# Padding the contraction of a small outer product from 32 rows to 128

## The reference

```
S_new = decay * S_old + outer(k, v_new)        # k, v_new: 128 values each, S: 128 x 128
```

## Time and profile before

| | before |
|---|---|
| median of 3 runs | 1237.82 us |
| lowest and highest | 1236.69 and 1238.21 us |
| span of the profiled execution | 1235.7 us |
| TensorE busy (weight loads) | 1207.5 us (1125.5 us) |
| VectorE, ScalarE, GpSimd busy | 793.9, 518.5, 303.2 us |
| mean granted TensorE clock | 0.995 |

### The profile page before, as it was taken

The page is one execution under the profiler, slowest core; times in us unless marked ns, Lnnn a source line. Parts: engine busy times, 40 slices in busy tenths (PEclk is TensorE's granted clock), DMA queues, the critical chain, the costliest instruction groups (busy, mean ns, idle before and its releaser), DMA issues.

```text
span 1235.7 us, 25524 instructions
## 1 busy us (share of the span) xinstructions
PE 1207.5 (98%) x8793; PEld 1125.5 (91%) x8793; DVE 793.9 (64%) x1944; ACT 518.5 (42%) x1376; POOL 303.2 (25%) x275
## 2 busy tenths in 40 slices
PE   5999999999999999999999999999999999999997
PEld 4899999999999999999999999999999998999996
DVE  5576577657765776567656765676567658365544
ACT  6453334533453345334533453345344535532211
POOL 1114122412241224112311232123212322222211
PEclk8999999999999999999999999999999999999999
DMA  7332443245314532443244314432443255232253
GB/s 243 99 94 63 140 164 104 63 141 163 103 63 141 163 103 63 140 164 103 63 148 156 103 62 146 158 103 63 150 154 103 89 195 193 87 102 71 98 205 140
DMA packets 79645, 151.55 MB, mean 123 GB/s; under 512 B 12353, under 2 KB 22242, under 8 KB 77986
## 3 DMA queue, kind: packets, MB, share of 16 engines
q1 hardware_dynamic: 78254, 148.78, 38.1%
q10 hardware_dynamic: 1312, 1.59, 0.5%
HBM read 132.20 MB, written 17.27 MB: 121 GB/s over the span
## 4 chain that ended last, share of the span: by engine, by line
PE 82%; DVE 8%; ACT 4%; issue 3%; DMA 1%; SPq 0%; DVEq 0%; ACTq 0%
PE PJ L611 17%; PE PJ L607 11%; PE PJ L608 10%; PE PJ L609 10%; PE PJ L612 9%; PE MX L817 3%; PE MX L798 2%; DVE memx L1574 1%; PE PJ L930 1%; PE MX L809 1%; PE MX L741 1%; PE PJ L931 1%; PE PJ L932 1%; PE MX L721 1%; PE MD L869 1%
## 5 line engine op out<-in xcount | busy, mean ns | idle before, releaser
L1962 POOL TENSOR_TENSOR w_lo<-w_raw,w_hi 128x512 fp32r<-128x512 f32 x160 | 217.9, 1362 | 814.0 <-ACT w_hi L1003 814.0
L611 PE MATMUL PJ<-h,w_hi 128*128 128x512 f32 x1110 | 416.8, 412 | 0.0
L607 PE MATMUL PJ<-h,w_hi 128*128 128x264 f32 (+1 forms) x1216 | 356.6, 293 | 0.0
L608 PE MATMUL PJ<-h,w_hi 128*128 128x264 f32 (+1 forms) x1216 | 344.7, 283 | 0.0
L609 PE MATMUL PJ<-h,w_lo 128*128 128x264 f32 (+1 forms) x1216 | 344.6, 283 | 0.0
L612 PE MATMUL PJ<-h,w_lo 128*128 128x256 f32 x1110 | 310.7, 280 | 0.0
L611 PEld LDWEIGHTS PJ<-h,w_hi 128*128 128x128 f32 x1110 | 209.0, 188 | 43.3 <-DVE w_lo L1381 1.7
L1003 ACT ACTIVATE w_hi<-w_raw 128x512 fp32r<-128x512 f32 x320 | 196.6, 624 | 91.3 <-PE PJ L609 79.1
L607 PEld LDWEIGHTS PJ<-h,w_hi 128*128 128x128 f32 x1216 | 229.3, 189 | 4.0 <-issue 3.9
L608 PEld LDWEIGHTS PJ<-h,w_hi 128*128 128x128 f32 x1216 | 229.6, 189 | 1.6
L609 PEld LDWEIGHTS PJ<-h,w_lo 128*128 128x128 f32 x1216 | 228.3, 188 | 0.0
(11 more groups left out here) (333 smaller groups left out, 1840.5 us busy)
## 6 DMA issues: line engine op xcount, KB each, us to landing
w_raw<-in_w_in SPq DMA_DIRECT2D x256, 256.0 KB, 2.7
w_raw<-in_w_out SPq DMA_DIRECT2D x64, 256.0 KB, 2.9
kv<-in_cache_win_k SPq DMA_DIRECT2D x24, 512.0 KB, 4.6
kv<-in_cache_win_v SPq DMA_DIRECT2D x16, 512.0 KB, 4.7
out<-memx SPq DMA_DIRECT2D x16, 260.0 KB, 4.7
mem<-in_x_prompt SPq DMA_DIRECT2D x4, 1024.0 KB, 10.1
S<-in_state_delta SPq DMA_DIRECT2D x8, 512.0 KB, 3.4
out<-S SPq DMA_DIRECT2D x8, 512.0 KB, 2.9
```

The source lines that it names most:

```text
L607: pe.matmul(ps, wh, h_hi[:, k, tok], start=k == 0, stop=False)
L608: pe.matmul(ps, wh, h_lo[:, k, tok], start=False, stop=False)
L611: pe.matmul(both, wh, h2[:, :, k, tok], start=k == 0, stop=False)
L1962: pool.tensor_tensor(w_lo[:, par, 4 * q:4 * q + 4, :], w_raw[:, q, :, :], w_hi[:, par, 4 * q:4 * q + 4, :].bitcast(F32), ALU.subtract).the ...
```

## The change

The tile `rt` is made 128 rows high under the name `rt_all`. `rt` becomes its first 32 rows, so that all that writes or reads it stays as it was, `kvr` and `vexp` too. Rows 32 to 127 are set to zero once, by a memset of the whole tile on VectorE at the start, between the two that are there. L887 now takes all 128 rows of both operands: the 96 rows of zeros add nothing to the sum.

```diff
-        rt = sb("rt", [4 * NB, 6 * P], F32R)
+        rt_all = sb("rt_all", [P, 6 * P], F32R)
+        rt = rt_all[0:4 * NB, :]
+        vexp_all = rt_all[:, 0:4 * P]
+        kvr_all = rt_all[:, 4 * P:6 * P].rearrange("p (n t) -> p n t", n=2)
         vexp = rt[:, 0:4 * P].rearrange("p (b e) -> p b e", e=P)
         pd = rb[0:NB, P:4 * P].rearrange("p (n t) -> p n t", n=3)
         kvr = rt[:, 4 * P:6 * P].rearrange("p (n t) -> p n t", n=2)
...
-                    pe.matmul(MD[:, 1, :], kvr[:, 0, :], vexp.rearrange("p b e -> p (b e)"), start=True,
+                    pe.matmul(MD[:, 1, :], kvr_all[:, 0, :], vexp_all, start=True,
                               stop=True).then_inc(s["d_outer"], 1)
...
             dve.memset(gt, 0.0)
+            dve.memset(rt_all[:].bitcast(F32), 0.0)
             dve.memset(ones[:], 1.0).then_inc(s["memset_ok"], 1)
```

## The result

| | before | changed |
|---|---|---|
| median of 9 runs each | 1236.69 us (1234.62 to 1240.15) | 1231.15 us (1229.34 to 1233.02) |
| ratio, 95% interval | | 0.9948 (0.9935 to 0.9961) |
| profiled execution | span 1235.7 us | time 1230.87 us, span 1229.0 us |

The change makes the kernel faster by 0.52%, between 0.39% and 0.65%, by the ratio on record. That ratio equals the one of the first three runs of each kernel (medians 1231.32 and 1237.82 us); the two medians of nine in the table give 0.9955, 5.5 us.

The account below looks back on a forecast made before the run. TensorE, busy 98% of the span, was taken as the bound. Sixteen pairs saving 0.34 us each make 5.4, with nothing for the memset: 1237.82 - 5.4 = 1232.4 us; 8-in-10 range 1231.0 to 1235.3, forecast's own 1231.0 to 1233.8.

Parts of the forecast that it names:

- TensorE's stream is the bound, and what leaves it leaves the span: TensorE is busy 857.4 of 858.8 us around the edited products, so time saved there should shorten the span almost whole.
- The price today: At L887, one 32-row product costs 0.58 us of TensorE's time; 512 columns cost a projection product 0.23.
- The new price: In the chain, 128-row L887 takes 0.29 us and L607 behind it 0.12: pair 0.41 against 0.75, 0.34 saved.
- Both ends mend: Entry to L887 (0.43 to 0.29) and exit at L607 (0.32 to 0.12) both get cheaper, 5.4 us over sixteen.
- The page that speaks against it: Skill rule that a single 32-row matmul takes as long as a 128-row one; by it L887's change saves 0.3 us.
- The memset: Added VectorE memset of 128 x 768 at the start: estimated 0.70 us, hidden by a transfer wait until 9.21 us.
- The next wait: After L817, L798 comes 0.34 us sooner, covered by 1.1 us of slack; then L853 waits for L1694, 0.20 us.
- One end only: Rival at L887 and L607: entry alone gives 1235.6 us (chance 0.03), exit alone 1234.6 us (chance 0.05).
- No effect: Rival at L887: its bank or the waits in front cost, not its row count; 1237.5 to 1238.5 us, chance 0.05.
- A wait that takes it: Rival: VectorE's L1694 comes no earlier, so L853 gives back 0.68 us in seven heads; 1237.2 us, chance 0.04.
- The clock: Rival: more rows switching drops TensorE's granted clock in the projection behind each product; 18 us added, 1250, chance 0.04.
- best bound: At best the new L887 costs 0.23 us, the pair 0.35; 6.4 us saved over sixteen products, giving 1231.4 us.

Follow-up runs that it names:

- the second measurement: The changed kernel run again with no edit, against the kernel before: 1230.93 us against 1236.5 us, ratio 0.9955 (0.9942 to 0.9967).

## Why the prediction was right, and where it was off

*TensorE's stream is the bound, and what leaves it leaves the span.* Right. The first and last starts of the sixteen products moved by the sum of what the products between them gave up, to within 0.2 us.

*The price today, 0.58 us a product, of which 0.23 is the columns' own.* Right; the doubled product measures the 0.23 directly.

*The new price, 0.29 and 0.12.* Right to the hundredth, all sixteen times. The nearest row, L611 behind the same eight pieces, was the right one: same columns, same type, same neighbours, and only the row count different.

*Both ends mend.* Right. Neither end alone was the case. The support from the 8-row group was weaker than it looked: with full-row products in front, the four transposes still take 0.50, so of the 0.16 that was read there as an excess on leaving (0.60 against 0.44), 0.10 was one.

*The page that speaks against it.* The Trainium skill's rule, in "TensorE: Matmul & The Clock Gate", section "Why this matters for your kernels", that a single product over 32 rows takes the time of one over 128, holds for the durations (498 and 480 ns) and for a second product in a row (0.23 us in either form). It isn't the whole price in a stream of full-row products. The Trainium skill's "TensorEngine Tiling (Array Packing)", section "Key Properties", gives a reason for the missing part, the drain at a change of mode. The late weight loads fit it, and so does that 64 rows pay and 96 don't: under "Tiling Modes" the same page lists row tilings of 64 and 32 rows, beside none. No record of these profiles shows a mode or a drain as such, so the reason stays the page's.

*The memset.* Estimated at 0.70 us, measured 0.70, hidden.

*The next wait.* The slack of 1.1 us at L798 held, and the seven waits at L853 stayed at 0.2.

*The rivals.* One end only: fell, by the chain. No effect: fell with 64 against 96 rows. A wait that takes it: fell, by the waits. The clock: the granted clock stayed at 1.00 in the stretch with the sixteen products, and the changed kernel is not slower.

*The step that failed* is the last one, the level under the sum and the noise in its range. The prediction took the median of three runs, 1237.82 us, as the level, by holding the 2.1 us above one profiled span as fixed: 1237.82 - 5.4 = 1232.4. Over nine runs the median before is 1236.69, 1.1 us lower; 5.4 from there is 1231.3, 0.1 from the measured 1231.15. So the saving was sized rightly (5.5 us between the medians of nine, 5.6 in the second measurement) and the stated 1232.4 is 1.3 us high because of the level.

The range has the same fault, and its low end doesn't follow from its own terms. The noise was put at 0.8 us around the median of the three runs, but the lowest of them, 1236.69, lies 1.1 below it; and the best bound less 0.8 is 1231.4 - 0.8 = 1230.6, not 1231.0. The median of nine, 1231.15, is only just inside the range, and the profiled execution of the changed kernel, 1230.87, lies outside it. That the median falls inside is in part luck.

What the runs showed in place of 0.8 us: the nine runs of the kernel before lie up to 3.5 us from their median (1234.62 to 1240.15). The profiles name sources of it. The wait at L930 was 0, 1.0 or 1.3 us; a stretch at the lower clock behind it, 1.2 us at the end of the span, came in one profile of nine; and the start varies too, as the first of the sixteen products starts between 119.7 and 121.9 us in the nine profiles, in either kind of kernel. Two profiles of the changed kernel have the same span, 1229.0 us, by such chance: the second starts its first product 1.8 us later and has no wait at the end. The extra 1.3 us in the pair of profiles is of that kind. What decides the length of the wait, the clock behind it and the start was not tried.

## What to carry to other kernels

A small product that uses a quarter or half of the array's rows, put alone into a dense stream of full ones, costs more than its columns: here 0.34 us of 0.58, nearly invisible in its own duration, and seen in the weight loads, which come late at both of its ends. Read such a price from the pieces of the chain or from start to start, beside the same place without the product, and look for the same columns with full rows nearby for the price after. Pad with zeros where the count of instructions and the weight loads stay the same; where padding turns cheap small operations into more or longer ones, as with the 8-row transposes, the ends saved don't pay for it.

## What the hardware showed that was not expected

The step lies between 64 and 96 rows: 64 rows cost as much as 32 (pair 0.75 us), 96 as little as 128 (0.41). And a second 32-row product directly behind the first costs 0.23 us, so that two of them in one place share one way in and one way out.

The granted clock fell to its lower level for some three microseconds at the output projection in one profile of nine, behind a wait of 1.3 us; in another kernel's profile the same wait of 1.3 us left it at full.
